# Up projections by seven half-size products: one change to a two-block kernel on one core

## The chip, the cores and the metric

One Trainium2 chip, one of its cores. The metric is the device time of one execution in microseconds (us). Everything is float32. The kernel before takes 2658.76 us (median of three runs, 2657.78 to 2661.27).

## The reference, cut to what matters

The program computes two transformer blocks one after the other on 256 tokens of width 1024. The second block puts 16 extra tokens in front (272 in all) and has two layers, each a mixer followed by a feed-forward layer. The change touches the two feed-forward layers and nothing else in the mathematics:

```
def conv_ffn(u, w_up, conv_w, conv_b, w_down):
    h = causal_dwconv(u @ w_up, conv_w, conv_b)
    g, up = jnp.split(h, 2, axis=-1)
    return (jax.nn.gelu(g, approximate=True) * up) @ w_down
```

Here u is 272 x 1024, w_up 1024 x 5632, w_down 2816 x 1024, and the convolution has three taps along the tokens, for each column by itself.

## The kernel before, in words

Activations are kept transposed: 128 channels on the partitions, tokens along the free dimension. Weights come from HBM in units of 1 MB (128 partitions x 2048 numbers) into a ring of six slots (`ring`, `R = 6`). SyncE issues the transfers in program order; the transfer of unit u waits until TensorE has counted unit u-6 as used (`unit_used`).

An up projection has 22 units (`FT`). A unit holds, for each of the eight blocks of 128 input channels, 256 output columns: 128 of the gate half and the 128 of the linear half that belong to them. TensorE makes two tiles of a unit, c=0 and c=1, each of eight accumulating matmuls with 128x128 weights and all tokens of the layer as moving columns (272 in the first layer, 258 in the second, where the first 14 tokens are no longer needed). That is `project`, line 543. The two tiles alternate between banks 6 and 7 of PSUM. The first unit of a layer, `pre_unit` (line 2575), runs on activations that aren't normalised yet, between the row sums of the norm (line 2545).

Per tile, ScalarE copies the bank to `up` (line 1200), and VectorE runs the convolution on it: `conv` is one tensor_scalar (line 1775) and two scalar_tensor_tensor (line 1777), both scalar_tensor_tensor reading two operands in SBUF. When both tiles of unit j have been convolved, ScalarE makes the gelu (line 1208) and VectorE, one unit later, the product with the linear half (`gated`, line 1791) into `actF`. Then the down projection (`project_deep`, line 573) takes two ring units per output tile and eleven matmuls from each.

Ahead of an up projection stands the norm of the mixer's result. GpSimd adds up six of its eight tiles of squares (`add_squares`, line 2036) and TensorE, ScalarE and VectorE finish it: reciprocal (line 607), `post_norm` (lines 1766 and 1769, sixteen tensor_tensor on SBUF operands), ScalarE's `pre_tiles` (lines 1174 and 1175), TensorE's `pre_unit`, and again a reciprocal and eight products into `ub` (`pre_norm`, line 1756). During an up projection GpSimd has nothing to do.

Each engine runs its own list in the order in which it is written; they meet at semaphores only. On VectorE, `chain` makes the next instruction wait for the one before it.

## Time and profile before

| | us |
|---|---|
| median of three runs | 2658.76 |
| the profiled execution | 2658.56 |
| its span, first to last instruction | 2656.7 |
| TensorE busy in the span | 2405.3 |
| VectorE busy | 761.1 |
| ScalarE busy | 560.0 |
| GpSimd busy | 48.8 |

The span is what the trace covers; the 1.9 us between it and the execution's own time lie around it. Busy time is the time in which an engine has at least one instruction in work. TensorE's instructions overlap, so the distance from one to the next, not the duration of one, gives its pace. A float32 matmul of the program stands in the trace as two MATMUL instructions, each with its weight load.

### The profile page before, as it was taken

What the parts mean: (1) busy time and instruction counts of PE and PEld (TensorE: products, weight loads), DVE (VectorE), ACT (ScalarE), POOL (GpSimd) and SP (SyncE); (2) the same over time, 40 slices, a digit from 0 to 9 for tenths busy, and PEclk for the clock granted to TensorE, in tenths of its full rate; (3) what the DMA queues carried; (4) which work ended last, traced back from release to release, by engine and by line L of the source; (5) the groups of instructions that cost most, each with busy time, mean ns of one, the idle gap of its engine ahead of it and who ended that gap; (6) DMA issues with size and microseconds to landing.
All of it is one profiled execution on the core that took longest, in us unless ns stands there. A gap on an engine that the chain in (4) does not pass through costs nothing.

```text
span 2656.7 us, 36561 instructions
## 1 busy us (share of the span) xinstructions
PE 2405.3 (91%) x15194; PEld 1591.4 (60%) x15194; DVE 761.1 (29%) x1852; ACT 560.0 (21%) x1411; POOL 48.8 (2%) x69
## 2 busy tenths in 40 slices
PE   6999997899997988989887768989999999999998
PEld 4685875587442433433432225767888788677887
DVE  1010355632121111111111103652441325724431
ACT  2110112511121211211111113441111221522110
POOL 0000000000000000000000000100000000110000
PEclk9999999898999999999998898999999999999999
DMA  8132243045999999899999996323334343123432
GB/s 324 64 124 82 80 190 143 16 152 219 370 403 420 406 420 421 350 420 420 421 420 420 421 421 262 117 80 111 143 128 135 138 147 135 64 80 127 156 122 87
DMA packets 86936, 608.38 MB, mean 229 GB/s; under 512 B 9552, under 2 KB 11728, under 8 KB 16080
## 3 DMA queue, kind: packets, MB, share of 16 engines
q1 hardware_dynamic: 86224, 602.49, 57.8%
q8 instruction: 123, 2.02, 0.3%
q0 software_dynamic: 400, 2.46, 0.2%
q10 hardware_dynamic: 144, 1.05, 0.1%
q14 instruction: 45, 0.37, 0.0%
HBM read 604.91 MB, written 1.05 MB: 228 GB/s over the span
## 4 chain that ended last, share of the span: by engine, by line
PE 72%; SPq 11%; DMA 10%; DVE 4%; ACT 2%; issue 2%; DVEq 0%; POOL 0%; ACTq 0%
PE bank L543 29%; SPq L843 11%; PE bank L573 10%; PE bank L2391 8%; DMA arena<-in_w_e 6%; PE bank L557 4%; PE bank L2412 4%; DMA ring<-in_w_e 3%; PE bank L2152 2%; PE bank L2339 2%; PE bank L2575 1%; PE bank L2178 1%; PE bank L2355 1%; DMA ring<-in_w_ada 1%; PE bank L2631 1%
## 5 line engine op out<-in xcount | busy, mean ns | idle before, releaser
L543 PE MATMUL bank<-arena,ring 128*128 128x272 f32 (+3 forms) x3200 | 762.5, 400 | 4.5 <-ACT arena L897 2.0
L543 PEld LDWEIGHTS bank<-arena,ring 128*128 128x128 f32 x3200 | 608.4, 191 | 150.6 <-issue 51.6
L2391 PE MATMUL bank<-arena 128*32 128x512 f32 x2184 | 279.2, 626 | 49.5 <-DMA arena<-in_w_e 49.4
L573 PE MATMUL bank<-arena,ring 128*128 128x272 f32 (+2 forms) x1216 | 273.6, 388 | 0.0
L573 PEld LDWEIGHTS bank<-arena,ring 128*128 128x128 f32 x1216 | 231.9, 191 | 41.3 <-issue 1.2
L1660 DVE TENSOR_TENSOR arena<-bank,arena 128x256 f32<-128x256 f32 x56 | 23.8, 424 | 795.5 <-PE bank L2368 770.4
L2391 PE MATMUL bank<-ring,arena 128*32 128x512 f32 x1400 | 180.8, 627 | 39.6 <-DMA ring<-in_w_e 37.7
L2391 PEld LDWEIGHTS bank<-arena 128*32 128x32 f32 x2184 | 60.0, 111 | 201.5 <-DMA arena<-in_w_e 100.9
L1777 DVE SCALAR_TENSOR_TENSOR arena<-arena,par 128x272 f32<-128x272 f32 (+1 forms) x296 | 148.8, 503 | 10.5
L2412 PE MATMUL bank<-arena 128*32 128x256 f32 x1824 | 118.9, 407 | 30.0 <-DMA arena<-in_w_e 25.9
L1073 ACT ACTIVATE arena<-bank 32x256 f32<-32x256 f32 x224 | 84.0, 375 | 252.1 <-PE bank L2412 249.7
L2412 PE MATMUL bank<-ring,arena 128*32 128x256 f32 x1760 | 109.6, 395 | 25.8 <-DMA ring<-in_w_e 19.2
L2391 PEld LDWEIGHTS bank<-ring,arena 128*32 128x32 f32 x1400 | 38.1, 111 | 141.3 <-DMA ring<-in_w_e 81.5
L2412 PEld LDWEIGHTS bank<-arena 128*32 128x32 f32 x1824 | 61.5, 115 | 92.1 <-DMA arena<-in_w_e 34.5
L1775 DVE TENSOR_SCALAR arena<-arena,par 128x272 f32<-128x272 f32 (+1 forms) x128 | 53.5, 418 | 218.4 <-ACT arena L1200 155.8
L557 PE MATMUL bank<-ring,arena 128*128 128x256 f32 x512 | 113.3, 379 | 0.0
L2412 PEld LDWEIGHTS bank<-ring,arena 128*32 128x32 f32 x1760 | 58.6, 113 | 79.5 <-issue 26.8
L557 PEld LDWEIGHTS bank<-ring,arena 128*128 128x128 f32 x512 | 97.3, 190 | 14.1 <-issue 1.0
L607 DVE RECIPROCAL arena<-arena 128x272 f32<-128x272 f32 (+2 forms) x8 | 14.5, 1818 | 299.1 <-ACT arena L601 287.4
L1087 ACT ACTIVATE arena<-bank 128x512 f32<-128x512 f32 x56 | 33.3, 597 | 267.3 <-PE bank L2391 262.3
L1200 ACT ACTIVATE arena<-bank 128x272 f32<-128x272 f32 (+1 forms) x84 | 32.9, 392 | 259.0 <-PE bank L543 259.0
L1186 ACT ACTIVATE arena<-bank 128x272 f32<-128x272 f32 (+2 forms) x32 | 12.5, 391 | 249.5 <-PE bank L573 249.5
(423 smaller groups left out, 2139.2 us busy)
## 6 DMA issues: line engine op xcount, KB each, us to landing
arena<-in_w_e SPq DMA_DIRECT2D x222, 1024.0 KB, 25.7
ring<-in_w_e SPq DMA_DIRECT2D x162, 1024.0 KB, 25.9
ring<-in_w_up SPq DMA_DIRECT2D x44, 1024.0 KB, 4.8
ring<-in_w_l SPq DMA_DIRECT2D x37, 1024.0 KB, 4.8
ring<-in_w_ada SPq DMA_DIRECT2D x24, 1024.0 KB, 6.3
ring<-in_w_proj SPq DMA_DIRECT2D x24, 1024.0 KB, 4.8
ring<-in_w_down SPq DMA_DIRECT2D x32, 704.0 KB, 4.0
ring<-in_w_merge SPq DMA_DIRECT2D x16, 1024.0 KB, 5.0
```

Of the source, the lines that this page charges most:

```text
L543: mm = pe.matmul(o[:, a:n], ring[:, s, k * 256 + c * P:k * 256 + (c + 1) * P], rhs(k), start=(k == 0), stop=(k == KT - 1))
L557: mm = pe.matmul(o[:, 0:256], lhs(k, t), ring[:, s, k * 256:(k + 1) * 256], start=(k == 0), stop=(k == KT - 1))
L573: mm = pe.matmul(o[:, a:n], ring[:, s, k * P:(k + 1) * P], rhs(part * kt + k), start=(part == 0 and k == 0), stop=(part == parts - 1 and k ...
L843: sp.dma_start(slot(s), dram[name][bass.ds(known[at], 1), c, :, :].rearrange("a p n -> (a p) n"))\
L1073: ins = act.activation(ys[j * GROUP:(j + 1) * GROUP, (g // QUAD) % 2, q * 256:(q + 1) * 256], bank[q * GROUP:(q + 1) * GROUP, b, col:col + ...
L1087: act.activation(ht[:, g % 2, :], bank[:, hidden_bank(g), :], ACT.Copy).then_inc(sem("ht_ready"), 1)
L1775: chain(dve.tensor_scalar(dst, src[:, a:L], w(0), b, ALU.mult, ALU.add))
L1777: ins = dve.scalar_tensor_tensor(out=dst, in0=src[:, a + k:k + L], scalar=w(k), in1=dst, op0=ALU.mult, op1=ALU.add)
L2152: mm = pe.matmul(o, ring[:, s, k * 256 + n % 2 * P:k * 256 + (n % 2 + 1) * P], u_lat(k), start=(k == 0), stop=(k == KT - 1))
L2339: mm = pe.matmul(bank[:, at_bank, (k % 2) * 256 + lead:(k % 2 + 1) * 256], u2tok[:, t, k * P:(k + 1) * P], sel[:, c % 2, t, lead:], start= ...
L2391: mm = pe.matmul(bank[q * GROUP:(q + 1) * GROUP, hidden_bank(g), :], xe[:, (g // CHUNK) % 2, k, s:s + GROUP], w[:, q * 512:(q + 1) * 512], ...
L2412: mm = pe.matmul(bank[q * GROUP:(q + 1) * GROUP, b, col:col + 256], hidden, w[:, c * D + q * 256:c * D + (q + 1) * 256], start=(k == 0 and ...
```

## The change

Of the 22 units of each up projection the first two stay as they were (`PLAIN = 2`). For the other twenty, a unit's weights are seen as two by two blocks: even and odd input blocks (j) by gate and linear columns (c), four matrices a11, a12, a21, a22 of four 128x128 blocks each. The activations are seen as two by two likewise: even and odd input blocks by the first and the second half of the tokens (h = 136 or 129 columns). The product of two such matrices is made from seven half-width products instead of eight:

- VectorE makes four sums of the activations once per layer (`unit_halves`), each 128 x 4 x h.
- GpSimd makes four sums of the weights per unit (`weight_sums`), each a tensor_tensor of 128 x 512, into one of three buffers (`SUMS = 3`). It waits for the unit's transfer and, for the buffer, until TensorE has used the unit three before.
- TensorE (`project_seven`) makes seven products of four accumulating matmuls each, with h moving columns, into three banks; two sets of three banks alternate. It waits for each sum, and before unit n for VectorE's having read unit n-2 (`seven_read`).
- ScalarE copies the first product to both token halves of the gate row (one instruction per unit where there were two).
- VectorE adds the other six products from PSUM in four tensor_tensor (`seven_tiles`), and then runs both convolutions as before.

```diff
--- before.py
+++ after.py
@@ -349,6 +349,9 @@
 LAST_PHASE = 5
 DECAYS = 6
 MERGE0 = (56, 48, 80)
+PLAIN = 2
+SUMS = 3
+SEVEN_BANKS = ((0, 1, 2), (3, 4, 5))
 
 
 class Chain:
@@ -448,8 +451,9 @@
         stream += units_of("w_merge", 3, 16) + units_of("w_out", 0, 4)
         MOE0 = len(stream)
         EU = 12
-        tail = []
+        tail, first_unit = [], {}
         for name in ("w_l0", "w_l0o", "w_up0", "w_down0", "w_l1", "w_l1o", "w_up1", "w_down1"):
+            first_unit[name] = MOE0 + len(tail)
             tail += [(dram[name][n], dram[name].shape[2]) for n in range(dram[name].shape[0])]
         TAIL0 = MOE0
 
@@ -545,6 +549,50 @@
                     mm.then_inc(sem("tile_done") if c == 0 else sem("unit_used"), 1)
                     if behind is not None:
                         behind(2 * unit + c)
+                at.unit += 1
+
+        def quarters(s):
+
+            v = ring[:, s, :].rearrange("p (q j c m) -> p c j q m", q=KT // 2, j=2, c=2)
+            return v[:, 0, 0], v[:, 0, 1], v[:, 1, 0], v[:, 1, 1]
+
+        def halves(x, j, l, a):
+
+            h = (L - a) // 2
+            return x.rearrange("p (q j) t -> p q j t", j=2)[:, :, j, a + l * h:a + (l + 1) * h]
+
+        def project_seven(pe, at, n_units, a):
+
+            h = (L - a) // 2
+            b11, b21, b22 = halves(ub, 0, 0, a), halves(ub, 1, 0, a), halves(ub, 1, 1, a)
+            for unit in range(n_units):
+                s = slot_filled(pe, at)
+                n, at.seven = at.seven, at.seven + 1
+                a11, a12, a21, a22 = quarters(s)
+                low, mid, high = SEVEN_BANKS[n % 2]
+                if n >= 2:
+                    pe.wait_ge(sem("seven_read"), n - 1)
+
+                def product(b, part, w, x):
+                    for q in range(KT // 2):
+                        mm = pe.matmul(bank[:, b, part * h:(part + 1) * h], w[:, q, :], x[:, q, 0:h],
+                                       start=(q == 0), stop=(q == KT // 2 - 1))
+                    return mm
+
+                product(low, 0, a11, b11)
+                product(low, 1, a12, b21)
+                if unit == 0:
+                    at.sums += 1
+                    pe.wait_ge(sem("halves_ready"), at.sums)
+                product(high, 1, a22, usum[:, 3])
+                pe.wait_ge(sem("sums_ready"), 4 * n + 1)
+                product(mid, 1, wsum[:, n % SUMS, 0, :].rearrange("p (q m) -> p q m", m=P), usum[:, 0])
+                pe.wait_ge(sem("sums_ready"), 4 * n + 2)
+                product(mid, 0, wsum[:, n % SUMS, 2, :].rearrange("p (q m) -> p q m", m=P), usum[:, 2])
+                pe.wait_ge(sem("sums_ready"), 4 * n + 3)
+                product(low, 2, wsum[:, n % SUMS, 1, :].rearrange("p (q m) -> p q m", m=P), usum[:, 1])
+                pe.wait_ge(sem("sums_ready"), 4 * n + 4)
+                product(high, 0, wsum[:, n % SUMS, 3, :].rearrange("p (q m) -> p q m", m=P), b22).then_inc(sem("unit_used"), 1)
                 at.unit += 1
 
         def project_tokens(pe, at, n_units, lhs, tiles, behind=None):
@@ -765,6 +813,8 @@
         cv = take(2, 2, L)
         gl = take(2, L)
         actF = take(FT, L)
+        wsum = take(SUMS, 4, UW // 4)
+        usum = take(4, KT // 2, L // 2, at=27136)
         Place.at = second
         zs = take(ST, L)
         xb = take(CT, L)
@@ -1187,12 +1237,26 @@
                     act.activation(ym[:, k, a:], o[:, a:L], ACT.Copy, scale=prm(g, k)).then_inc(free, 1)
                 norm_root(act, at, rsb[:, a:], L, D, a)
 
+            at.seven = 0
+
+            def seven_first(b, a):
+
+                h = (L - a) // 2
+                low = SEVEN_BANKS[at.seven % 2][0]
+                at.seven += 1
+                at.unit += 1
+                act.wait_ge(sem("unit_used"), at.unit)
+                act.activation(up[:, b, 0, 2 + a:].rearrange("p (l t) -> p l t", l=2),
+                               bank[:, low, 0:h].unsqueeze(1).to_broadcast([P, 2, h]), ACT.Copy).then_inc(sem("seven_first"), 1)
+
             def ffn(n, a=0, a2=0):
                 pre_tiles(f"f{n}_pre", a)
                 for j in range(FT):
                     if j >= 2:
                         act.wait_ge(sem("ffn_conv"), at.ffn + j - 1)
-                    for c in range(2):
+                    if j >= PLAIN:
+                        seven_first(j % 2, a)
+                    for c in range(2 if j < PLAIN else 0):
                         if j == 0:
                             tile_skip(at, c == 1)
                         else:
@@ -1781,10 +1845,47 @@
                     else:
                         ins.then_inc(last, 1)
 
+            at.seven = 0
+
+            def unit_halves(a):
+
+                h = (L - a) // 2
+                b11, b12, b21, b22 = halves(ub, 0, 0, a), halves(ub, 0, 1, a), halves(ub, 1, 0, a), halves(ub, 1, 1, a)
+                at.ub += KT
+                dve.wait_ge(sem("ub_ready"), at.ub)
+                chain(dve.tensor_tensor(usum[:, 0, :, 0:h], b12, b11, ALU.subtract))
+                dve.tensor_tensor(usum[:, 2, :, 0:h], b22, b12, ALU.subtract)
+                chain(dve.tensor_tensor(usum[:, 1, :, 0:h], b22, usum[:, 0, :, 0:h], ALU.subtract))
+                dve.tensor_tensor(usum[:, 3, :, 0:h], b21, usum[:, 1, :, 0:h], ALU.subtract).then_inc(sem("halves_ready"), 1)
+
+            def seven_tiles(b, a):
+
+                h = (L - a) // 2
+                n, at.seven = at.seven, at.seven + 1
+                low, mid, high = SEVEN_BANKS[n % 2]
+                at.unit += 1
+                dve.wait_ge(sem("seven_first"), at.seven)
+                v = up[:, b, :, 2 + a:].rearrange("p c (l t) -> p c l t", l=2)
+                start = second + 2 * b * (L + 2) + 2 + a + h
+                inner = arena[:, start:start + 2 * (L + 2 - h)].rearrange("p (x t) -> p x t", x=2)[:, :, 0:h]
+
+                def two(b, part):
+                    return bank[:, b, part * h:(part + 2) * h].rearrange("p (x t) -> p x t", x=2)
+
+                def both(b, part):
+                    return bank[:, b, part * h:(part + 1) * h].unsqueeze(1).to_broadcast([P, 2, h])
+
+                chain(dve.tensor_tensor(v[:, 0], v[:, 0], two(low, 1), ALU.add))
+                chain(dve.tensor_tensor(v[:, 1, 0], v[:, 0, 1], bank[:, mid, 0:h], ALU.add))
+                chain(dve.tensor_tensor(v[:, :, 1], inner, both(mid, 1), ALU.add))
+                dve.tensor_tensor(inner, inner, two(high, 0), ALU.add).then_inc(sem("seven_read"), 1)
+                dve.wait_ge(sem("seven_read"), at.seven)
+
             def ffn(n, a=0, a2=0):
                 at0 = at.out
                 chain(dve.memset(up[:, :, :, 0:2], 0.0))
                 pre_norm(lambda c: up[:, 0, c, 2 + a:], a)
+                unit_halves(a)
 
                 def gated(j):
                     dve.wait_ge(sem("ffn_gelu"), at.ffn + j + 1)
@@ -1795,9 +1896,11 @@
                     for c in range(2):
                         if j == 0:
                             dve.wait_ge(sem(f"bank_read{(at0 + c) % NL}"), (at0 + c) // NL + 1)
-                        else:
+                        elif j < PLAIN:
                             o, free = tile_out(dve, at, c == 1)
                             dve.wait_ge(free, (at.out + 1) // NL)
+                        elif c == 0:
+                            seven_tiles(j % 2, a)
                         i = 2 * j + c
                         conv(cv[:, j % 2, c, a2:], up[:, j % 2, c, :], lambda k: prm(f"f{n}_cw", k * 44 + i),
                              prm(f"f{n}_cb", i), 3, sem("ffn_conv") if c == 1 else None, a2)
@@ -1807,6 +1910,7 @@
                 at.ffn += FT
 
             at.ffn = 0
+            at.ub = KT
             at.unit = TAIL0
             at0 = at.out
             chain(dve.memset(xr[:, :, 0:3], 0.0))
@@ -1899,6 +2003,7 @@
             chain(dve.memset(xp[:, :, 0:3], 0.0))
             chain(dve.memset(csr[:, :], 0.0))
             pre_norm(lambda c: zs[:, c, LATE:], 0, LATE)
+            at.ub += KT
             dve.wait_ge(sem("dt_step"), 1)
             dve.tensor_scalar(dtr[0:SH, :], bank[0:SH, 4, 0:L], prm("dt_bias")[0:SH, :], None, ALU.add)\
                .then_inc(sem("dt_step"), 1)
@@ -2037,13 +2142,33 @@
                     pool.wait_ge(sem("square_part"), (KT - 2) * step + k)
                 pool.nop().then_inc(sem("square_sum"), 1)
 
+            def weight_sums(name, count):
+
+                for unit in range(first_unit[name] + PLAIN, first_unit[name] + FT):
+                    a11, a12, a21, a22 = quarters(unit % R)
+                    s1, s2, s3, s4 = [wsum[:, count % SUMS, i, :].rearrange("p (q m) -> p q m", m=P) for i in range(4)]
+                    pool.wait_ge(sem(f"filled{unit % R}"), 16 * (unit // R + 1))
+                    if count >= SUMS:
+                        before = unit - SUMS + 1 if unit - SUMS >= first_unit[name] + PLAIN else first_unit["w_down0"]
+                        pool.wait_ge(sem("unit_used"), before)
+                    pool.tensor_tensor(s1, a21, a22, ALU.add).then_inc(sem("sums_ready"), 1)
+                    pool.tensor_tensor(s3, a11, a21, ALU.subtract).then_inc(sem("sums_ready"), 1)
+                    pool.wait_ge(sem("sums_ready"), 4 * count + 1)
+                    pool.tensor_tensor(s2, s1, a11, ALU.subtract).then_inc(sem("sums_ready"), 1)
+                    pool.wait_ge(sem("sums_ready"), 4 * count + 3)
+                    pool.tensor_tensor(s4, a12, s2, ALU.subtract).then_inc(sem("sums_ready"), 1)
+                    count += 1
+                return count
+
             add_squares(0, 5 * KT)
+            summed = weight_sums("w_up0", 0)
             add_squares(1, 7 * KT)
             phase(pool, 5)
             for n in range(ST):
                 pool.wait_ge(sem("ssm_y_read"), n + 1)
                 pool.tensor_tensor(zs[:, n, LATE:], zs[:, n, LATE:], xb[:, n, LATE:], ALU.mult).then_inc(sem("ssm_gated"), 1)
             add_squares(2, 9 * KT + ST, LATE)
+            weight_sums("w_up1", summed)
             add_squares(3, 11 * KT + ST, LAST)
 
 
@@ -2582,14 +2707,15 @@
 
             def ffn(a=0, a2=0):
                 pre_unit(a)
-                project(pe, at, FT - 1, lambda k: ub[:, k, a:], L, first=ub_first, a=a)
+                project(pe, at, PLAIN - 1, lambda k: ub[:, k, a:], L, first=ub_first, a=a)
                 at.ub += KT
+                project_seven(pe, at, FT - PLAIN, a)
                 at.ffn += FT
                 at.a = a2
                 project_deep(pe, at, 2, FT // 2, lambda k: actF[:, k, a2:], L, done=result_sum, a=a2,
                              first=lambda k: pe.wait_ge(sem("ffn_act"), at.ffn - FT + k + 1))
 
-            at.ub = at.ffn = at.a = at.post = 0
+            at.ub = at.ffn = at.a = at.post = at.seven = at.sums = 0
 
             def lru_gates(n):
                 pe.wait_ge(sem("xc_ready"), n + 1)
```

## Rows read from the trace of the kernel before

**Rows 1.** The page's first part: busy time of each engine.

```profile
PE 2405.3 (91%) x15194; PEld 1591.4 (60%) x15194; DVE 761.1 (29%) x1852; ACT 560.0 (21%) x1411; POOL 48.8 (2%) x69
```

**Rows 2.** Both up projections' line-543 stretches: busy per engine, granted clock, DMA share.

```profile
core 0: us, PE busy (x) PEld busy (x) DVE busy (x) ACT busy (x) POOL busy (x), PEclk, DMA share, GB/s
1852.16:2006.18 154.02, 154.02 (x673) 127.70 (x673) 70.83 (x157) 24.06 (x62) 0.00 (x0) 1.00 0.38 133
2422.45:2568.68 146.23, 146.23 (x673) 127.75 (x673) 68.56 (x157) 23.32 (x62) 0.00 (x0) 1.00 0.40 140
```

**Rows 3.** Waits inside the first up projection: who, for whom, total, times, longest.

```profile
ACT arena L1200 <- PE bank L543: 133.1, 42, 6.9
DVE arena L1775 <- ACT arena L1200: 80.7, 41, 2.1
```

**Rows 4.** VectorE's instruction groups in the two up projections, by form.

```profile
L1777 DVE SCALAR_TENSOR_TENSOR arena<-arena,par 128x272 f32<-128x272 f32 x76 | 38.2, 502 | 2.7
L1775 DVE TENSOR_SCALAR arena<-arena,par 128x272 f32<-128x272 f32 x38 | 16.0, 421 | 75.8 <-ACT arena L1200 75.8
L1791 DVE TENSOR_TENSOR arena<-arena 128x272 f32<-128x272 f32 x19 | 8.2, 434 | 0.0
...
L1777 DVE SCALAR_TENSOR_TENSOR arena<-arena,par 128x256 f32<-128x256 f32 x76 | 36.8, 484 | 2.7
```

**Rows 5.** Timeline of TensorE about the 128-column matmuls of line 2621.

```profile
1701.56 1.54 PE L2616 MATMUL bank<-arena,ring 128*128 128x272 f32 x6
1702.93 5.58 PE L2621 MATMUL bank<-ring,arena 128*128 128x128 f32 x48
1708.44 0.50 PE L2631 MATMUL bank<-arena,ring 128*128 128x272 f32 x1
```

**Rows 6.** GpSimd's tensor_tensor groups by form: count, busy, mean ns.

```profile
L2036 POOL TENSOR_TENSOR arena<-arena 128x272 f32<-128x272 f32 x12 | 9.1, 758 | 329.5 <-ACT arena L1186 329.5
...
L2036 POOL TENSOR_TENSOR arena<-arena 128x256 f32<-128x256 f32 x6 | 4.3, 725 | 233.1 <-ACT arena L1186 233.1
```

**Rows 7.** Timeline of VectorE, then of GpSimd, from 1708.6 to 1711.9 us.

```profile
1708.01 0.72 DVE L1843 TENSOR_TENSOR_SCAN arena<-arena 128x272 f32<-128x272 f32 x1
1708.66 0.41 DVE L1842 TENSOR_TENSOR arena<-arena 128x272 f32<-128x272 f32 x1
1709.11 1.17 DVE L1843 TENSOR_TENSOR_SCAN arena<-arena 128x272 f32<-128x272 f32 x1
...
1708.82 0.88 POOL L2030 TENSOR_TENSOR arena<-arena 128x272 f32<-128x272 f32 x1 [25.91 <-DVE arena L1843]
```

**Rows 8.** Timeline of GpSimd and VectorE about line 1835.

```profile
1682.14 0.76 POOL L2026 TENSOR_TENSOR arena<-arena 128x272 f32<-128x272 f32 x1 [3.82 <-ACT arena L1221]
1682.66 0.40 DVE L1835 TENSOR_SCALAR arena<-arena 128x272 f32<-128x272 f32 x1 [9.59 <-ACT arena L1242]
...
1685.34 0.29 DVE L1835 TENSOR_SCALAR arena<-arena 128x272 f32<-128x272 f32 x1
```

**Rows 9.** Lines 1957 and 1969, with GpSimd's line 2045 beside them: min/median/max ns.

```profile
L1957 DVE TENSOR_TENSOR arena<-bank,csp x32: 444/452/459, 2289.3 to 2332.0; 128x288 f32<-128x288 f32 x32
...
L1969 DVE TENSOR_TENSOR arena<-arena x32: 574/583/1118, 2292.1 to 2333.8; 128x416 f32<-128x416 f32 x32
...
L2045 POOL TENSOR_TENSOR arena<-arena 128x258 f32<-128x258 f32 x16 | 12.0, 751 | 247.1 <-DVE arena L1975 247.1
```

**Rows 10.** Timeline of VectorE and ScalarE after the first units of the up projection.

```profile
1856.22 0.42 DVE L1775 TENSOR_SCALAR arena<-arena,par 128x272 f32<-128x272 f32 x1
1856.67 1.04 DVE L1777 SCALAR_TENSOR_TENSOR arena<-arena,par 128x272 f32<-128x272 f32 x2
1857.63 0.41 DVE L1775 TENSOR_SCALAR arena<-arena,par 128x272 f32<-128x272 f32 x1
...
1859.71 0.40 ACT L1200 ACTIVATE arena<-bank 128x272 f32<-128x272 f32 x1 [3.27 <-PE bank L543]
```

**Rows 11.** Timeline from GpSimd's last sum of squares to the first up projection.

```profile
1825.93 0.76 POOL L2036 TENSOR_TENSOR arena<-arena 128x272 f32<-128x272 f32 x1 [6.58 <-ACT arena L1186]
...
1836.41 0.79 DVE L1766 TENSOR_TENSOR arena<-arena 128x272 f32<-128x272 f32 x2
...
1841.35 0.79 DVE L1769 TENSOR_TENSOR hT<-hT,arena 128x272 f32<-128x272 f32 x2
...
1843.14 0.42 ACT L1175 ACTIVATE arena<-hT 128x272 f32<-128x272 f32 x1
...
1847.57 1.08 PE L2545 MATMUL bank<-arena,con 128*128 128x272 f32 x4
```

**Rows 12.** Transfers of the up projection's weights: KB each, us to landing.

```profile
ring<-in_w_up SPq DMA_DIRECT2D x44, 1024.0 KB, 4.8
```

**Rows 13.** Two stretches in which TensorE has gaps: as rows 2.

```profile
1382.00:1407.00 25.00, 20.37 (x168) 7.85 (x160) 3.88 (x16) 3.11 (x7) 0.00 (x0) 0.86 1.01 420
...
2302.00:2352.00 50.00, 45.59 (x314) 28.02 (x311) 38.45 (x81) 27.56 (x84) 10.24 (x14) 0.93 0.01 1
```

## The prediction

> **What bounds the kernel now.** The page's busy times come first: TensorE works in 91% of the span, no other engine in more than 29%, and GpSimd in 2% [rows 1]. So a change that takes matmul time away and puts work on GpSimd and VectorE looks sound; whether it is must be read from the stage. The two stretches of line 543 have TensorE busy all the time, at the full granted clock (2.4 GHz), with VectorE busy for under half and GpSimd for none of it [rows 2]. The waits agree: ScalarE waits for TensorE and VectorE for ScalarE, 42 and 41 times, and TensorE for nobody [rows 3]. A unit is 32 MATMUL instructions, so it takes 154.0/21 = 7.33 us in the first layer and 146.2/21 = 6.96 us in the second. These are the prices of before: 20 units each, 146.7 and 139.3 us.
>
> **TensorE's side of the change.** A unit becomes 7 products x 4 matmuls x 2 = 56 instructions of 136 or 129 columns. The pace at 272 columns is 229 ns an instruction (154.0/672). For short ones the nearest row is line 2621: 48 instructions of 128 columns in 5.51 us from the first start to the next group (1702.93 to 1708.44), 0.115 us each [rows 5], although their weight loads are as large as here. Between 115 ns and half of 229 at 136 columns lies nothing, so I take 0.116 us: 56 x 0.116 = 6.50 us a unit; for 129 columns 0.112 us and 6.27. If nothing else were late the change would save 20 x 0.83 + 20 x 0.69 = 30 us. The bounds: no saving from shorter columns below 0.115 in either layer makes the second unit 6.44 us and costs 3 us of that. Six satisfied waits a unit instead of two I price at nothing: across the two tile borders of a unit the pace of 229 ns shows no gap. The upper bound is 0.05 us for each of the four more, 0.2 us a unit. The transfers need 4.8 us of the 6.3 and stay hidden [rows 12].
>
> **GpSimd's side.** Its tensor_tensor takes 725 ns for 256 columns and 758 for 272 [rows 6]: 2.06 ns a column and about 0.20 us fixed, so 1.25 us for the 512 of a weight sum. That is the lower bound; in proportion to 272 columns it would be 1.43, the upper. I take 1.26. Four a unit make 5.0 us, with their waits about 5.3: below 6.5, so by itself GpSimd would keep up, three units ahead.
>
> **VectorE's side, alone.** Before, a unit costs it two convolutions and a gated product. By the timeline, a tensor_scalar starts 1.41 to 1.53 us before the next one [rows 10], and the product adds 0.4 [rows 4]: 3.35 us. New are four tensor_tensor from PSUM in a chain: three over 272 columns at 0.44 (the row has 0.452 for 288 [rows 9]) and one over 136 at 0.30, with 0.035 between them: 1.76 us. Together 5.1 us, again below 6.5. ScalarE's 0.40 us copy [rows 10] stands ahead of the chain, behind the unit's last matmul.
>
> **The two together.** Now the row that decides. GpSimd's tensor_tensor starts at 1708.82 and lasts 0.88 where 0.76 is usual; VectorE's tensor_tensor on SBUF operands had run until 1709.07. So GpSimd waited for its end: it would have taken hold 0.14 us after its start. VectorE's scan, issued at 1709.11, lasts 1.17 where it lasts 0.72 elsewhere: it began in effect at 1709.56, 0.14 us ahead of GpSimd's end [rows 7]. Line 1835 shows the same for a tensor_scalar in SBUF: 0.40 instead of 0.29, from 0.13 us ahead of GpSimd's end [rows 8]. Line 1969 (two SBUF operands) goes from 583 up to 1118 ns, line 1957 (one operand from PSUM), beside the same GpSimd work, only from 444 to 459 [rows 9]. So the two engines exclude each other for all of a unit's seven convolution and gating instructions, and not for the four additions from PSUM. A sum of 512 columns holds from 0.14 after its start to 0.14 before its end: 1.26 - 0.28 = 0.98 us. One that meets a waiting VectorE costs it 0.98 less some of the gap between its instructions, 0.90 us.
>
> The Trainium skill (SBUF — State Buffer, Who interferes with whom) says that GpSimd and a VectorE instruction with two SBUF inputs or in a two-port mode share a pair of ports under an exclusive lock held for the whole instruction. This case's rows agree on the exclusion and differ on its length, which ends 0.14 us early; the lock for a whole instruction would be 1.26 us for each sum, and is the fourth rival's upper end.
>
> Where the four sums fall: GpSimd's next burst starts when TensorE has used a unit (its buffer comes free), takes hold at +0.2, and again every 0.98 + 0.34. Assume VectorE is the late one; then TensorE starts a unit when VectorE has ended the additions of two units ago (time 0) and ends it at 6.6. VectorE's period is T, its additions run from T-1.8 to T. With T = 7.9: the first sum holds 6.8 to 7.8, beside the additions, free. The tensor_scalar gets in at 7.93 to 8.35; the second sum holds 8.35 to 9.33, the scalar_tensor_tensor follows, the third holds 9.76 to 10.74, the fourth 11.17 to 12.15. Three meet VectorE: T = 5.1 + 3 x 0.90 = 7.8. With T put in at 7.6 or 8.3 the same list gives 8.0 and 7.6. So T = 7.85, above the 7.33 of before. For the second layer 0.2 less, 7.65 against 6.96.
>
> **The sum.** Layer 0, from the end of the last plain unit: the first additions end at 6.5 + 0.5 + 1.8 = 8.8. TensorE can run ahead of VectorE by two units only; two transient periods of 9 us (there the bursts of two units meet the same convolutions) bring the third additions to 27; fourteen more periods to 27 + 14 x 7.85 = 137, when the last unit but one may start. Two units of 6.5 and a short wait: 150. Against 146.7: +3.5 us. Layer 1: 26.5 + 14 x 7.65 = 133.6, + 12.8 = 146.4, against 139.3: +7 us. The down projection takes the last `actF` only at its 22nd k, 10 us in, as 22 x 0.46; VectorE needs about 7 (copy 0.4, additions 1.8, convolutions 3.0, gelu and product 0.4 each, and waits): nothing.
>
> Ahead of each up projection: `unit_halves` is four tensor_tensor over 544 columns, 0.72 us each by 583 ns for 416 columns [rows 9], 3 us in all; its last sum is needed after one plain unit and two products, 9.2 us after the first `ub`, and is there after 7. Nothing; with no cover it would be 3 us each. GpSimd ends its squares at 1826.7 and needs some 16 us for the twelve sums of three units, but VectorE starts `post_norm` at 1836.4, so four or five sums meet its sixteen instructions and make them end 4 to 5 us later. TensorE ended this passage at 1848.6, 5 us behind ScalarE's last 1843.6 [rows 11], so most of that is covered: +1 us each (0 to 5), +2.
>
> Sum: 2658.56 + 3.5 + 7 + 2 = 2671 us for the profiled execution, which stands 0.2 us from the median of the runs. TensorE then idles 1.3 us a unit. In a stretch with 9% gaps the clock was granted at 0.93, with 19% at 0.86 [rows 13]; at 0.93 a unit of 6.5 becomes 7.0, still under 7.85. Price nothing, with an upper end of 8 us.
>
> **Rivals.** (1) TensorE stays the bound: VectorE meets fewer than 1.5 sums a unit, (6.5 - 5.1)/0.90, because GpSimd's sums fall beside additions and gaps. For it: both engines alone fit. Against: GpSimd's own 5.3 us against 1.8 us of additions. Then 2658.6 - 30 + 2 = 2631, faster. It is the case on the other side. (2) Two sums meet, T = 7.0 to 7.3 in layer 0 and 0.2 less in layer 1, no long transient: 28 periods x 0.7 less, 20 us less than forecast: 2651. (3) The weight loads bind: 190 ns each if they didn't overlap, 56 x 0.19 = 10.6 us a unit, +140 us, 2799. Against: rows 5, where as large loads pass every 0.115. (4) A longer hold: 1.43 us for a sum adds 0.17 x 3 to each of 28 periods, +14, 2685; the hold of a whole instruction adds 0.28 x 3 x 28 = +24, 2695. For it: no row has 512 columns or operands in blocks of 128.
>
> **How the numbers follow.** Forecast 0.50 (2671, its own range 2660 to 2682); (1) 0.18; (2) 0.13; (3) 0.02; (4) 0.17. What can be told from no change is 0.2%, 5.3 us. Faster: all of (1), two thirds of (2), a little of the forecast's low side: 0.30. Same: the rest of (2) and the forecast's lower edge: 0.10. Slower: 0.60. The range that leaves out (3), part of (4) and half of (1): 2630 to 2697.
>
> **What would show it.** Right: in the up projections line 1777 has a mean well over 502 ns, 0.6 to 0.75 us, while the new additions keep 0.44; TensorE's idle time there is released by VectorE's last addition; GpSimd's sums take 1.3 to 1.6 us; units start every 7.8 us. TensorE's short instructions follow at 0.116 us inside a product. Wrong: TensorE busy without gaps through the forty units, or waiting on GpSimd's sums, or line 1777 at 502 ns.

## The result, and the profile after

The changed kernel takes 2675.63 us (median of five runs, 2673.45 to 2680.96) against 2658.76 of the kernel before: ratio 1.007, 95% interval 1.0053 to 1.0087. It is slower, by 17 us or 0.7%; 2671 had been forecast. The profiled execution has a span of 2672.7 us, 16.0 more than before. From here on a "period" is the time from one seven-product unit to the next on TensorE, and a "passage" the time from a mixer's last matmuls to the first plain unit of the up projection.

The page's first part, as [rows 1]:

```profile
PE 2373.8 (89%) x16154; PEld 1600.7 (60%) x16154; DVE 930.2 (35%) x2020; ACT 548.3 (21%) x1371; POOL 260.5 (10%) x229
```

TensorE's busy time fell by 31.5 us, 24.0 of them in the up projections, and the kernel is longer all the same. The stretches say where. First and third the passages, second and fourth the up projections, with the columns of [rows 2]:

```profile
1829.10:1852.54 23.44, 14.70 (x54) 10.68 (x52) 15.43 (x22) 7.82 (x20) 10.24 (x8) 0.78 0.13 45
1852.54:2009.71 157.17, 140.65 (x1153) 136.81 (x1153) 147.79 (x234) 18.14 (x42) 90.61 (x68) 1.00 0.38 131
2407.90:2431.55 23.65, 14.85 (x54) 11.18 (x53) 15.19 (x22) 7.59 (x20) 10.30 (x8) 0.78 0.12 44
2431.55:2584.63 153.08, 135.65 (x1154) 132.34 (x1154) 143.92 (x234) 17.64 (x42) 89.99 (x68) 1.00 0.39 134
```

The up projections take 157.2 and 153.1 us instead of 154.0 and 146.2 [rows 2], with VectorE busy for 94% of each instead of 46 and 47%; together +10 us. The passages took 19.6 and 17.9 us before (same view, 1832.52 to 1852.16 and 2404.60 to 2422.45) and take 23.4 and 23.7: together +9.6 us. The sum is 19.6; the span grew by 3.6 us less than that. Most of the difference lies where both kernels do the same: the experts' matmuls start 3.8 us earlier in the profiled execution (at 650.8 instead of 654.6 us) and take as long as before (941.6 and 941.5 us).

Who is waited for in the first up projection now, as [rows 3]:

```profile
ACT arena L1272 <- DVE arena L1841: 98.4, 18, 6.3
POOL arena L2154 <- PE bank L578: 61.9, 17, 27.2
ACT arena L1249 <- PE bank L578: 28.9, 19, 5.8
...
PE bank L578 <- DVE arena L1881: 16.5, 15, 1.3
```

TensorE, which waited for nobody, waits 15 times for VectorE's last addition (line 1881). The groups of the same stretch, as [rows 4], show why VectorE is late:

```profile
L1841 DVE SCALAR_TENSOR_TENSOR arena<-arena,par 128x272 f32<-128x272 f32 x82 | 70.6, 861 | 2.9
L1839 DVE TENSOR_SCALAR arena<-arena,par 128x272 f32<-128x272 f32 x40 | 32.4, 810 | 1.4
L2157 POOL TENSOR_TENSOR arena<-arena,ring 128x512 f32<-128x512 f32 x17 | 24.8, 1459 | 0.0
L2159 POOL TENSOR_TENSOR arena<-ring,arena 128x512 f32<-128x512 f32 x17 | 22.9, 1346 | 1.3
L2155 POOL TENSOR_TENSOR arena<-ring 128x512 f32<-128x512 f32 x17 | 22.6, 1332 | 0.0
L2154 POOL TENSOR_TENSOR arena<-ring 128x512 f32<-128x512 f32 x17 | 21.7, 1274 | 61.9 <-PE bank L578 61.9
...
L1881 DVE TENSOR_TENSOR arena<-arena,bank 128x272 f32<-128x272 f32 x19 | 8.3, 437 | 0.7
```

The convolutions' instructions (lines 1839 and 1841 are the old 1775 and 1777) went from 421 and 502 ns to 810 and 861, while the additions from PSUM take 437. One period in the timeline, VectorE first, then GpSimd:

```profile
1933.55 0.44 DVE L1881 TENSOR_TENSOR arena<-arena,bank 128x272 f32<-128x272 f32 x1
1934.02 0.43 DVE L1839 TENSOR_SCALAR arena<-arena,par 128x272 f32<-128x272 f32 x1
1934.49 2.82 DVE L1841 SCALAR_TENSOR_TENSOR arena<-arena,par 128x272 f32<-128x272 f32 x2
1937.34 1.25 DVE L1839 TENSOR_SCALAR arena<-arena,par 128x272 f32<-128x272 f32 x1
1938.63 1.04 DVE L1841 SCALAR_TENSOR_TENSOR arena<-arena,par 128x272 f32<-128x272 f32 x2
...
1933.03 1.26 POOL L2154 TENSOR_TENSOR arena<-ring 128x512 f32<-128x512 f32 x1 [2.25 <-PE bank L578]
1934.25 1.32 POOL L2155 TENSOR_TENSOR arena<-ring 128x512 f32<-128x512 f32 x1
1935.54 1.47 POOL L2157 TENSOR_TENSOR arena<-arena,ring 128x512 f32<-128x512 f32 x1
1937.09 1.35 POOL L2159 TENSOR_TENSOR arena<-ring,arena 128x512 f32<-128x512 f32 x1
```

In this period GpSimd's first sum lies beside the additions and costs nobody anything. Each of the other three meets one instruction of VectorE: two scalar_tensor_tensor take 2.82 us together where they take 1.04 in the last row of VectorE, and one tensor_scalar 1.25 where it takes 0.43: 1.8 and 0.8 us, 2.6 in all. It is the list of the prediction, one instruction after the other. In every second period the burst starts a little later against VectorE, and the first sum also costs the first tensor_scalar 0.3 us (it takes 0.75 or 0.76): these are the longer of two periods that take turns, 7.97 and 7.66 us.

### The profile page after: what moved, and what is told of

Same layout as the page of the kernel before. It is cut to its first block, busy times and chain, and to the rows that moved or that the text cites. A ratio compares the mean times of both kernels' runs of the same rounds, so it can differ in the third digit from the quotient of the medians.

```text
span 2672.7 us, 38724 instructions
## 1 busy us (share of the span) xinstructions
PE 2373.8 (89%) x16154; PEld 1600.7 (60%) x16154; DVE 930.2 (35%) x2020; ACT 548.3 (21%) x1371; POOL 260.5 (10%) x229
## 4 chain that ended last, share of the span: by engine, by line
PE 61%; DVE 14%; SPq 12%; DMA 10%; ACT 2%; issue 2%; DVEq 0%; POOL 0%; ACTq 0%
PE bank L547 18%; SPq L893 11%; PE bank L621 10%; DMA arena<-in_w_e 8%; PE bank L2516 7%; DVE arena L1841 5%; PE bank L605 4%; PE bank L2537 3%; DVE arena L1839 2%; PE bank L2277 2%; DMA ring<-in_w_e 2%; PE bank L578 1%; PE bank L2464 1%; PE bank L2700 1%; PE bank L2303 1%
## 5 line engine op out<-in xcount | busy, mean ns | idle before, releaser
L547 PE MATMUL bank<-arena,ring 128*128 128x272 f32 (+3 forms) x1920 | 475.2, 408 | 6.7 <-ACT arena L947 4.1
L547 PEld LDWEIGHTS bank<-arena,ring 128*128 128x128 f32 x1920 | 364.8, 191 | 108.9 <-issue 52.5
L621 PEld LDWEIGHTS bank<-arena,ring 128*128 128x128 f32 x1216 | 233.8, 193 | 42.5 <-issue 1.6
L1841 DVE SCALAR_TENSOR_TENSOR arena<-arena,par 128x272 f32<-128x272 f32 (+1 forms) x296 | 207.6, 701 | 10.5
L578 PE MATMUL bank<-arena 128*128 128x136 f32 (+1 forms) x1280 | 152.1, 277 | 0.0
L578 PEld LDWEIGHTS bank<-arena 128*128 128x128 f32 x1280 | 148.7, 191 | 0.0
L578 PE MATMUL bank<-arena,ring 128*128 128x136 f32 (+1 forms) x960 | 118.0, 279 | 33.9 <-DVE arena L1881 33.9
L578 PEld LDWEIGHTS bank<-arena,ring 128*128 128x128 f32 x960 | 112.2, 191 | 39.1 <-issue 39.0
L2516 PEld LDWEIGHTS bank<-ring,arena 128*32 128x32 f32 x1400 | 37.8, 111 | 139.6 <-DMA ring<-in_w_e 79.9
L1839 DVE TENSOR_SCALAR arena<-arena,par 128x272 f32<-128x272 f32 (+1 forms) x128 | 84.0, 657 | 65.6 <-ACT arena L1403 42.9
```

The costliest lines, as they stand in the source:

```text
L547: mm = pe.matmul(o[:, a:n], ring[:, s, k * 256 + c * P:k * 256 + (c + 1) * P], rhs(k), start=(k == 0), stop=(k == KT - 1))
L578: mm = pe.matmul(bank[:, b, part * h:(part + 1) * h], w[:, q, :], x[:, q, 0:h], start=(q == 0), stop=(q == KT // 2 - 1))
L621: mm = pe.matmul(o[:, a:n], ring[:, s, k * P:(k + 1) * P], rhs(part * kt + k), start=(part == 0 and k == 0), stop=(part == parts - 1 and k ...
L1839: chain(dve.tensor_scalar(dst, src[:, a:L], w(0), b, ALU.mult, ALU.add))
L1841: ins = dve.scalar_tensor_tensor(out=dst, in0=src[:, a + k:k + L], scalar=w(k), in1=dst, op0=ALU.mult, op1=ALU.add)
L2516: mm = pe.matmul(bank[q * GROUP:(q + 1) * GROUP, hidden_bank(g), :], xe[:, (g // CHUNK) % 2, k, s:s + GROUP], w[:, q * 512:(q + 1) * 512], ...
```

## The experiments

All are compared with the kernel before, run on the same chip beside them (its medians there: 2657.5, 2657.4 and 2658.0 us). The changed kernel was not run again beside them, so a difference of a few us against its 2675.6 is read from the stages of the traces and not from the medians. Up projections and passages are taken from the traces as above. The edits are cut to the lines that matter; words behind # and the dots are put in here.

**hold_third.** The passage alone.

```diff
+                    if unit == first_unit[name] + PLAIN + 2:
+                        pool.wait_ge(sem("h_ready"), held)      # held: end of post_norm
                     pool.tensor_tensor(s1, a21, a22, ALU.add).then_inc(sem("sums_ready"), 1)
```

> GpSimd makes the first two units' sums as before, but waits with the third unit's four until post_norm has ended. Shared-access theory: the sixteen instructions of post_norm keep 0.43 us each in both layers (in the changed kernel four took 1.5 us), both passages from the mixer's last matmul to the first plain unit come back from 23.4 and 23.7 us towards 19.6 and 17.9, and the up projections stay at 157 and 153 us. Time 2667 us. Rival, that the passages were long because TensorE was granted the half clock there for 10 us by chance: VectorE comes back, but the time stays at 2672 to 2676.

2668.9 us, ratio 1.0038 (1.0023 to 1.0053), 6.7 us under the changed kernel; the intervals of the two ratios touch at 1.0053. The passages:

```profile
1829.66:1849.53 19.87, 14.76 (x53) 11.13 (x52) 11.16 (x22) 7.72 (x20) 9.68 (x8) 0.83 0.14 53
2405.03:2423.39 18.36, 13.22 (x54) 10.51 (x52) 10.91 (x22) 7.48 (x20) 9.72 (x8) 0.91 0.16 57
```

They came back by 3.6 and 5.3 us, and the up projections stayed at 157.15 and 153.06. In post_norm only the first two instructions are still late (1.52 us together instead of 0.79 [rows 11]), beside the second unit's last sum:

```profile
1833.55 1.52 DVE L1830 TENSOR_TENSOR arena<-arena 128x272 f32<-128x272 f32 x2
1835.00 0.43 DVE L1833 TENSOR_TENSOR hT<-hT,arena 128x272 f32<-128x272 f32 x1
1835.35 0.43 DVE L1830 TENSOR_TENSOR arena<-arena 128x272 f32<-128x272 f32 x1
```

So the passages' loss was GpSimd's third unit of sums. The clock followed: granted at 0.83 and 0.91 here and 0.83 and 0.90 in the kernel before, against 0.78 twice in the changed one. The rival, a half clock by chance, falls: the time came back to 2668.9, and in the traces of all ten kernels the two passages have 0.78 or 0.79 where the third unit's sums run into post_norm (the changed kernel, tiny_sums, write_only and sums_384) and 0.82 to 0.91 where they don't.

**tiny_sums.** GpSimd's instructions stay, their length goes.

```diff
+                    if unit - first_unit[name] - PLAIN >= SUMS:
+                        a11, a12, a21, a22, s1, s2, s3, s4 = [x[:, 0:1, 0:8] for x in (a11, a12, a21, a22, s1, s2, s3, s4)]
```

> From the fourth seven-product unit of a layer on, GpSimd's four sums have 8 columns instead of 512 (the rest of the sums is left out). Shared-access theory: VectorE needs 5.1 us a unit and TensorE is the bound at 6.50 and 6.26 us; the up projections take 138 and 132 us instead of 157 and 153, time 2636 us. Rival, that VectorE's own chain of seven additions and convolutions with its waits, or the wait of TensorE for VectorE, sets 7.8 us a unit whatever GpSimd does: 2670 to 2676 us.

2637.13 us, ratio 0.9919 (0.9898 to 0.994). Up projections 137.1 and 132.1 us, TensorE busy throughout:

```profile
1853.23:1990.30 137.07, 137.07 (x1153) 135.82 (x1153) 102.58 (x234) 16.09 (x42) 12.26 (x68) 1.00 0.43 150
2415.22:2547.30 132.08, 132.08 (x1153) 131.20 (x1153) 99.37 (x234) 15.58 (x42) 12.29 (x68) 1.00 0.44 156
```

VectorE's and TensorE's side of the change, with all their waits, fit. The length of GpSimd's sums alone costs 20.1 and 21.0 us in the two layers. The passages stay long here (23.6 and 23.7 us), since the third unit's sums have their full length.

**write_only.** GpSimd busy too, but reading nothing.

```diff
-                    pool.tensor_tensor(...)      # the four sums
+                        for i in range(4):
+                            half = wsum[:, count % SUMS, 2 * (i % 2):2 * (i % 2) + 2, :].rearrange("p a b -> p (a b)")
+                            ins = pool.memset(half, 0.0)      # chained by a semaphore
```

> From the fourth seven-product unit of a layer on, GpSimd makes four chained memsets of 1024 columns (about 0.97 us each) instead of the four sums, which are left out; it is as busy but reads nothing. Theory that VectorE's two-operand instructions wait for GpSimd's reads: the scalar_tensor_tensor keep 502 ns, the two tensor_scalar a unit may wait; VectorE stays under 6.5 us a unit and TensorE is the bound: 2636 to 2642 us. Rival, that any GpSimd work on SBUF shuts VectorE out: a hold of 0.7 us three times a unit, T = 5.1 + 1.9 = 7.0 us, 2650 to 2655 us, and scalar_tensor_tensor with a mean over 0.6 us.

2638.44 us, ratio 0.992 (0.99 to 0.9941); up projections 137.1 and 132.1. GpSimd is not quite as busy as meant: a burst of four memsets takes 4.0 us instead of some 5.4 for four sums, and in the first up projection it works for 65 us instead of 91. VectorE's and GpSimd's groups in the first:

```profile
L1841 DVE SCALAR_TENSOR_TENSOR arena<-arena,par 128x272 f32<-128x272 f32 x70 | 35.1, 502 | 2.5
L1839 DVE TENSOR_SCALAR arena<-arena,par 128x272 f32<-128x272 f32 x34 | 22.5, 663 | 1.2
L2166 POOL MEMSET arena<- 128x1024 f32 x60 | 57.1, 952 | 40.2 <-PE bank L578 36.7
```

A scalar_tensor_tensor beside a GpSimd that only writes keeps its 502 ns; in the timeline two of them lie beside the fourth memset of each burst. A tensor_scalar waits even then: the one of the two in a unit that meets a memset takes 0.97 us, which makes the mean 663 instead of 421. So two SBUF operands collide with GpSimd's reads, and the tensor_scalar with its writes too. The shorter burst leaves the first reading as it is, since it rests on instructions that do lie beside a memset. The Trainium skill (SBUF — State Buffer, Who interferes with whom) says that a VectorE instruction with two SBUF inputs contends with a GpSimd instruction that reads SBUF and not with one that only writes it, and that one in a two-port mode, which a tensor_scalar can enter, contends with GpSimd. The trace agrees on both kinds (502 and 0.97 us); no run here shows the mode itself. That the pair is held for a whole instruction stands there with the two-port mode; the prediction took it for both kinds.

**sums_384.** The dose.

```diff
+                    if unit - first_unit[name] - PLAIN >= SUMS:
+                        a11, a12, a21, a22, s1, s2, s3, s4 = [x[:, 0:3, :] for x in (a11, a12, a21, a22, s1, s2, s3, s4)]
```

> From the fourth seven-product unit of a layer on, each sum covers 384 of its 512 columns (the last block is left out): 0.99 us instead of 1.26, hold 0.71 instead of 0.98. Shared-access theory with three sums meeting VectorE: T falls by 3 x 0.27 = 0.8 us to 7.05 and 6.85 us; TensorE is then barely the later; time about 2653 us. Rival, that VectorE loses a fixed time per GpSimd instruction, not its length: T and the time stay, 2672 to 2676 us.

2646.99 us, ratio 0.995 (0.9933 to 0.9967). The expectation was off in layer 0, where all of TensorE's periods are 6.49 us (up projection 137.1). One unit there, VectorE first, then GpSimd:

```profile
1936.03 1.27 DVE L1892 TENSOR_TENSOR arena<-arena 128x272 f32<-128x272 f32 x1
1937.21 0.43 DVE L1878 TENSOR_TENSOR arena<-arena,bank 128x272 f32<-128x272 f32 x1
...
1939.41 1.66 DVE L1841 SCALAR_TENSOR_TENSOR arena<-arena,par 128x272 f32<-128x272 f32 x2
...
1935.99 1.00 POOL L2156 TENSOR_TENSOR arena<-ring 128x384 f32<-128x384 f32 x1 [2.25 <-PE bank L578]
1936.95 1.21 POOL L2157 TENSOR_TENSOR arena<-ring 128x384 f32<-128x384 f32 x1
1938.12 1.00 POOL L2159 TENSOR_TENSOR arena<-arena,ring 128x384 f32<-128x384 f32 x1
1939.20 1.03 POOL L2161 TENSOR_TENSOR arena<-ring,arena 128x384 f32<-128x384 f32 x1
```

The second and third sum lie beside the additions. The first costs the gated product 0.8 us and the fourth a scalar_tensor_tensor 0.6: two meetings where three had been reckoned. VectorE alone needs 5.04 us (its periods in the changed kernel once GpSimd has finished), and with these 1.5 it just fits into TensorE's unit. In layer 1, where TensorE needs only 6.25, they don't fit. VectorE's own periods (from one second addition to the next) are 6.3 to 7.5 us from the second on; TensorE, which may run two units ahead, still keeps 6.25 for ten periods, while VectorE's additions fall back from 1.3 to 5.6 us behind the start of its unit's last matmul, and only then waits: 6.9 and 7.26 in turn (up projection 138.7). The forecast of 6.85 to 7.05 holds about from there (7.08 on average). So TensorE's ten short periods say nothing of a loop in balance; they are the time in which VectorE used up TensorE's lead.

**tap_on_scalar.** Fewer instructions of VectorE for GpSimd to meet. Also with hold_third's edit.

```diff
# ScalarE, behind seven_first and the gelu
+                        for c in range(2):
+                            i = 2 * j + c
+                            act.activation(cv[:, j % 2, c, a2:], up[:, j % 2, c, a2:L], ACT.Identity,
+                                           bias=prm(f"f{n}_cb", i), scale=prm(f"f{n}_cw", i)).then_inc(sem("tap_done"), 1)
# VectorE, conv()
-                chain(dve.tensor_scalar(dst, src[:, a:L], w(0), b, ALU.mult, ALU.add))
+                if not tapped:
+                    chain(dve.tensor_scalar(dst, src[:, a:L], w(0), b, ALU.mult, ALU.add))
```

> With GpSimd held before the third unit's sums as in hold_third, ScalarE makes the first tap of both convolutions (scale and bias, from up to cv) in the twenty seven-product units, and VectorE makes the gated product of the unit before while it waits for it. VectorE alone then needs 4.2 us a unit. Shared-access theory, the list of holds from the end of TensorE's unit: two sums fall beside the additions, two meet VectorE, which is ready 6.3 us after the additions' start: TensorE stays the bound in layer 0 (137 us) and nearly in layer 1 (132 to 136 us), passages 20.1 and 18.6 us; time 2628 us, faster than both kernels. Rival, that with VectorE late three sums meet it again and it does not get out of that: T = 4.2 + 2.7 = 6.9 us, up projections 144 and 143 us, 2645 us.

2645.61 us, ratio 0.996 (0.9947 to 0.9973): faster than both kernels, but it was the rival that came true, in its time (2645) and its up projections (144.8 and 143.1 measured in a profiled execution of 2652.0 us). Its period did not: TensorE has eleven periods of 6.5 in layer 0 and seven of 6.25 in layer 1, then 7.9 and 7.1 in turn (7.7 and 7.0 in layer 1), where 6.9 had been put throughout. By the timeline four and three sums in turn meet VectorE then, and 4.2 + 3.8 and 4.2 + 2.9 us are 8.0 and 7.1. That the totals agree is partly luck. The list of holds had VectorE ready 6.3 us after its start, too close: its own periods are 7.6 and 6.6 us from the third on, it slid behind and stayed.

**sums_on_vector.** The second engine taken away: VectorE makes all four sums, two units ahead, in four `dve.tensor_tensor` with the operands of GpSimd's.

> VectorE makes the weight sums itself, two units ahead, and GpSimd none. Theory: four more tensor_tensor of 512 columns at 0.68 us and their waits make VectorE's period 5.1 + 2.9 = 8.0 and 7.8 us with no meeting of the two engines at all: as long as with the sums on GpSimd, so the second engine brought nothing; scalar_tensor_tensor at 502 ns. Up projections 157 and 153 us, passages back to 20 and 18.5, time 2668 us. Rival, that VectorE's gaps or TensorE's wait for the sums in the middle of a unit cost more than the list says: 8.5 us a unit and more, over 2680 us.

2669.26 us, ratio 1.0056 (1.0041 to 1.007). Periods 7.57 and 7.42 us instead of the 8.0 and 7.8 of the list (the sums take 684 ns as priced, but start before the instruction ahead of them has ended), up projections 154.8 and 151.6, passages 19.4 and 17.7. That is 6 us under the changed kernel, with ratios whose intervals overlap; by the stages the up projections are 2.3 and 1.5 us shorter and the passages 4.0 and 6.0. The passages come back with hold_third too, and its 2668.9 us is the same time. So giving the sums to GpSimd saved nothing: in the up projections it cost some 2 us a layer more than doing them on VectorE.

**tap_and_split and split_alone.** GpSimd keeps the first and third sum, VectorE makes the second and fourth; once with ScalarE's taps, once without.

```diff
-                    pool.tensor_tensor(s2, s1, a11, ALU.subtract).then_inc(sem("sums_ready"), 1)
-                    pool.tensor_tensor(s4, a12, s2, ALU.subtract).then_inc(sem("sums_ready"), 1)
# VectorE, behind the convolutions of a unit, for the unit two later
+                dve.tensor_tensor(s2, s1, a11, ALU.subtract).then_inc(sem("vector_sums"), 1)
+                dve.wait_ge(sem("vector_sums"), 2 * count + 1)
+                dve.tensor_tensor(s4, a12, s2, ALU.subtract).then_inc(sem("vector_sums"), 1)
```

> tap_on_scalar with the weight sums divided: GpSimd makes the first and third of a unit, VectorE the second and fourth, two units ahead. VectorE's own time is 4.2 + 1.4 = 5.6 us; the two sums of GpSimd's burst hold from 0.2 to 2.5 us after TensorE's unit, where VectorE makes its additions (0.5 to 2.3), so they cost it 0.2 us. VectorE stays early, under 6.5 and 6.25 us, and TensorE is the bound through all forty units: up projections 137 and 132 us, passages 20 and 18.5 us, 2627 us. Rival, that VectorE drifts late as in tap_on_scalar and then meets both: 5.6 + 1.8 = 7.4 us, 2645 us or more.

2628.3 us, ratio 0.9888 (0.9872 to 0.9905): 30 us faster than the kernel before, 47 faster than the changed one, and as expected. A unit's first sum lies beside the additions, the second costs the gated product 0.2 us. TensorE is busy without a gap in both layers, 137.1 and 132.1 us:

```profile
1849.94:1987.03 137.09, 137.09 (x1153) 135.84 (x1153) 118.17 (x236) 37.42 (x80) 42.58 (x34) 1.00 0.43 150
2402.74:2534.84 132.10, 132.10 (x1154) 131.22 (x1154) 116.26 (x236) 36.36 (x80) 42.76 (x34) 1.00 0.44 156
```

> The same division of the sums, with all taps left on VectorE: its own time is 5.1 + 1.4 = 6.5 us, with 0.2 for the burst just over TensorE's unit. It falls behind slowly and then meets one to two of the two sums: 6.5 us a unit at first, 7.4 to 7.8 later, up projections about 147 and 145 us, 2650 us. Rival, that fewer sums on GpSimd are enough: 137 and 133 us, 2628 us.

2675.26 us, ratio 1.0063 (1.0046 to 1.008): slower than either was expected. After five and four undisturbed periods and one between, TensorE's periods are 8.2 and 8.0 us, up projections 158.6 and 156.6. Waits of TensorE in the first (from 1890 to 2000 us):

```profile
PE bank L578 <- DVE arena L1893: 10.9, 13, 0.9
...
PE bank L578 <- DVE arena L1881: 4.1, 13, 0.3
```

Line 1893 is VectorE's own weight sum. A late VectorE now holds TensorE up in the middle of a unit too. In each period both of GpSimd's sums meet VectorE (a tensor_scalar takes 1.37 us, two scalar_tensor_tensor 1.93), 6.5 + 2 x 0.9 = 8.3, where one to two had been reckoned. That the new wait brings this about, by moving the unit's end and with it the burst, is argued and not shown. Half the work for GpSimd in the wrong place is no better than all of it.

## Why the prediction was right, point by point

- **TensorE's pace.** 0.116 and 0.112 us an instruction were taken; the starts in the changed trace lie 116 and 112 ns apart, and units that wait for nothing take 6.49 and 6.25 us against 6.50 and 6.27. The weight loads of 190 ns overlap, so rival 3 is out. The nearest row was worse support than the prediction says: of its 48 instructions only 32 have weight loads as large, and the mean of 0.115 holds one pause of 0.2 us. The 32 start 112 ns apart in that trace, so 0.112 for 129 columns, which lies under the 0.115 of the row, turned out right without a row for it.
- **GpSimd's sum.** 1.26 us was taken from a line through 256 and 272 columns; undisturbed ones take 1.26 to 1.27. The operands in blocks of 128 cost nothing, and rival 4's longer hold is out.
- **The meeting.** Three sums a period were to meet VectorE at 0.90 us each, T = 7.85 and 7.65. Measured are 7.97 and 7.66 in turn in layer 0 and 7.65 and 7.60 in layer 1. In the timeline the three cost 2.6 us, 0.87 each. Only the sign was put too low: the old line 1777 was to have a mean of 0.6 to 0.75 us and has 0.86. tiny_sums and write_only show that it is the reading of GpSimd's sums that costs, not VectorE's chain.
- **The start.** "Two transient periods of 9 us": VectorE's first two periods are 9.0 and 9.3 us, and TensorE begins to wait with the fifth unit. The up projections were put at 150 and 146.4 us behind the plain unit; they took 149.8 and 146.0.
- **Rival 1**, TensorE the bound, is what the kernel does when the meetings go: 2637 us with the passages still long, 2628 with both mended. It had been given 2631.
- **The term that was mis-sized** is the passage: "+1 us each (0 to 5)", measured 3.8 and 5.8, in layer 1 outside even its own range. The number of sums that meet post_norm (four to five) and VectorE's delay were right: post_norm ends 5.0 us later against its reciprocal (at 1843.67 with the reciprocal at 1831.07, 12.6 us; before at 1842.14 [rows 11] with the reciprocal at 1834.53, 7.6 us). The cover was misread. TensorE was 5 us behind ScalarE's last activation [rows 11] because its work starts with the first one, and the delay sits on the first. Before, then after:

```profile
1837.59 0.52 ACT L1174 ACTIVATE arena<-hT,par 128x272 f32<-128x272 f32 x1 [3.17 <-DVE hT L1769]
1838.26 2.15 PE L2575 MATMUL bank<-arena,ring 128*128 128x272 f32 x4 [4.36 <-ACT arena L1174]
...
1831.07 1.85 DVE L655 RECIPROCAL arena<-arena 128x272 f32<-128x272 f32 x1 [61.41 <-ACT arena L649]
1832.95 2.58 DVE L1830 TENSOR_TENSOR arena<-arena 128x272 f32<-128x272 f32 x2
1835.46 1.50 DVE L1833 TENSOR_TENSOR hT<-hT,arena 128x272 f32<-128x272 f32 x1
1836.99 0.52 ACT L1224 ACTIVATE arena<-hT,par 128x272 f32<-128x272 f32 x1 [6.02 <-DVE hT L1833]
1837.65 1.25 PE L2700 MATMUL bank<-arena,ring 128*128 128x272 f32 x2 [7.21 <-ACT arena L1224]
1840.40 1.27 PE L2700 MATMUL bank<-arena,ring 128*128 128x272 f32 x2 [1.50 <-ACT arena L1224]
```

  ScalarE's first `pre_tiles` instruction starts 5.9 us after the reciprocal instead of 3.1. TensorE waits 7.2 us for it instead of 4.4 (4.1 in layer 1) and another 1.5 us for the next: 4.4 and 4.6 us more idle time, which is the bulk of the loss. TensorE was granted the half clock, 1.2 GHz, for 10.2 us in both passages instead of 6.8 and 3.4, but much of that fell on the idle time: its busy time is 0.6 us less in the first passage and 1.2 us more in the second. hold_third takes most of both back (5.1 us of waiting, half clock for 6.8 and 3.4).
- **Luck in the total.** The touched stages cost 19.6 us where 12.5 had been forecast. That the profiled execution came out only 16.1 us longer and not nearer 2678 us is due to the 3.6 us that it was quicker elsewhere.
- **The clock in the up projections** was priced at nothing, and it was granted in full throughout, though TensorE idles for 1.2 to 1.5 us in each of the later periods.

## What to carry to other kernels

Before work is handed to an idle GpSimd, list what VectorE does in the same microseconds: VectorE's instructions with two SBUF operands and GpSimd's that read SBUF run one after the other, so their lengths add up, while additions with one operand in PSUM lay beside them for nothing. Look at where the burst starts: tied to the same event as VectorE's PSUM work it can be free, as in tap_and_split, but once VectorE has slipped it can meet every sum and not recover, so leave margin rather than a fit. Look at VectorE's own periods to see it slip, for TensorE's show it only once its lead of two units is gone. And a delay in front of a passage is covered by TensorE's backlog only where it falls behind TensorE's first instruction, not before it.

## What the runs showed of the hardware that had not been expected

A tensor_scalar with two per-partition scalars from SBUF waits also for a GpSimd memset (421 to 663 ns on average), a scalar_tensor_tensor doesn't (502). VectorE's reciprocal of 128x272 in SBUF, which has one operand, keeps its 1.85 us beside GpSimd's sums (at 1831.07 in the changed kernel; 1.85 before, with GpSimd idle), so of the work in SBUF not all waits.
